# A hybrid decoder trunk on one core: in the recurrence's first two steps, where ScalarE copies the next q and f, and where VectorE does the next front

## The chip, the cores and the metric

The kernel runs on one core of one Trainium2 chip. The metric is the device time of the whole program in microseconds (us), lower is better, with the median of three runs as the kernel's time. A profile was taken of one further execution.

## The reference, cut to what matters

Two layers; each has a mixer with two branches that read the same input: sliding-window attention, and a gated linear recurrence (HGRN2) with four heads of 128 x 128 state. There is one prompt of 2048 tokens and a batch of eight samples of eight tokens each, and every sample comes with recurrence states of its own.

```python
def _hgrn2(q, f_logit, i_in, lb, s0):
    ...
    def step(S, blk):
        qc, gc, kc, vc = blk
        G = jnp.cumsum(gc, axis=1)
        diff = G[:, :, None] - G[:, None, :]
        decay = jnp.exp(jnp.where(causal, diff, NEG_INF))
        A = jnp.einsum('bthd,bshd,btshd->bhts', qc, kc, decay)
        o = jnp.einsum('bhts,bshv->bthv', A, vc) + jnp.einsum('bthd,bhdv->bthv', qc * jnp.exp(G), S)
        G_last = G[:, -1]
        S_new = jnp.exp(G_last)[..., None] * S + jnp.einsum(
            'bshd,bshv->bhdv', kc * jnp.exp(G_last[:, None] - G), vc)
        return S_new, o
```

## The kernel before, in words

Each layer has three phases, one after the other with a barrier between them: attention, recurrence, output. Each phase writes one program per engine, in the order in which the code stands; semaphores join the engines. An instruction that waits holds up all that stands behind it on its engine.

The recurrence runs over 17 tiles of tokens: tile 0 holds the 64 tokens of the eight samples, tiles 1 to 16 the prompt. For a tile, TensorE (PE) computes four projections q, f, g and v of 24 matmuls each into the four banks of `Z` (`project`), and turns q and f (`transpose_qf`) after ScalarE has copied them to `zqf` (`copy_z`, line 1002). ScalarE and VectorE then make the gates' logarithms and their running sum `G` (`front_log`, `front_exp`, `front`), and the levels of `A` are made by VectorE, ScalarE, GpSimd (POOL) and PE in turn (`middle`, `level`). Behind the levels come the "ends" of a tile: VectorE writes `kh`, ScalarE takes the exponentials of `kh` and `qG` (lines 1050 and 1051), POOL multiplies both (lines 964 and 965), and PE turns `kh` (line 1358). ScalarE copies the result to `khT` (line 1056).

Tile 0 has a way of its own. PE's order there is: the projection of f of tile 1, the turning of `kh`, eight products of `A` with `v` (line 1435), half of g of tile 1, `transpose_qf(1)`, samples 0 and 1, the other half of g, samples 2 and 3, v of tile 1, q of tile 2, samples 4 to 7, f of tile 2. For one sample (`sample_states`) PE reads its old state in eight matmuls (line 1410) and makes its update in eight more (line 1420). VectorE masks `khT` to a sample's rows (`state_rows`, line 1241) and then blends update and old state (`new_dec`, line 1247). The old states lie in four buffers `s_dec`; SyncE (SP) stores and loads them in this order:

```python
for b in range(4):
    store_state(b)
for b in range(4):
    sp.wait_ge(sd_st[b], 16)
    load_state(b + 4)
```

`store_state(b)` waits until `new_dec(b)` is done, so that the load for sample 4 stands behind the stores of samples 0 to 3. PE's reading of sample 4 waits for that load.

Of the kernel before, what the change touches and what calls it, by code (L numbers as in the profile page):

```python
# [30 lines left out]
DEC_BATCH, DEC_SEQ = 8, 8  # L31
# [39 lines left out]
def wait(eng, sem, value):  # L71

    if not isinstance(value, int) or value > 0:
        eng.wait_ge(sem, value)
# [751 lines left out]
def recurrence_phase(nc, layer, C, dram, S, weights, following):  # L826
# [4 lines left out]
    with ExitStack() as ctx:  # L831
# [37 lines left out]
        def first(n):  # L869

            return isinstance(n, int) and n == 0

        def tokens(n):

            return DEC if first(n) else P

        def passed(n):

            return 0 if first(n) else NL * n + len(DEC_LEVELS) - NL
# [6 lines left out]
        with nc.Block() as block:  # L886
# [106 lines left out]
            def _(act):  # L993
                def split_high(n, k):
                    act.wait_ge(S["x_in0"], 16 * n + 16)
                    wait(act, S["z_v"], n - 1)
                    act.activation(xh[k][:, :, :], xraw[:, :, :], ACT.Copy).then_inc(S["x_high"], 1)

                def copy_z(n):
                    act.wait_ge(S["z_f"], n + 1)  # L1000
                    wait(act, S["qf_ps"], n)
                    act.activation(zqf[:, :, :], Z[:, 0:1024], ACT.Copy).then_inc(S["zqf_sb"], 1)
# [6 lines left out]
                def front_log(n):  # L1009

                    act.wait_ge(S["z_g"], n + 1)
                    act.wait_ge(S["qf_ps"], n + 1)
                    wait(act, S["logf_done"], n)
                    act.activation(expo[:, :, :], FG, ACT.Abs).then_inc(S["act_abs"], 1)
                    act.wait_ge(S["act_abs"], n + 1)
                    act.activation(expo[:, :, :], expo[:, :, :], ACT.Exp, scale=-1.0).then_inc(S["act_exp"], 1)
                    act.wait_ge(S["act_exp"], n + 1)
                    act.activation(expo[:, :, :], expo[:, :, :], ACT.Ln, bias=1.0).then_inc(S["act_ln"], 1)
                    wait(act, S["ends_prod"], n)
                    wait(act, S["diag_ps"], n)  # L1020
                    act.activation(qT[:, :, :], banks["q"], ACT.Copy).then_inc(S["qT_sb"], 1)
# [12 lines left out]
                def middle(n, levels, after=lambda l: None):  # L1034
                    for l, h in enumerate(levels):
                        act.wait_ge(S["level_sub"], passed(n) + l + 1)
                        act.activation(E[l % 2][:, :], E[l % 2][:, :], ACT.Exp).then_inc(S["level_exp"], 1)  # L1037
                        if l == 3:
                            copy_uT(n - 1)
                        after(l)  # L1040
                    act.wait_ge(S["khx_done"], n + 1)
                    wait(act, S["o_done"], n)
                    if first(n):
                        last = G[:, :, 0:DEC].rearrange("p g (b t) -> p g b t", t=DEC_SEQ)[:, :, :, DEC_SEQ - 1]
                        act.activation(dec_s[:, :, :], last, ACT.Exp)
                    else:
                        wait(act, S["state_done"], n)
                        act.activation(decay[:, :], G[:, :, P - 1], ACT.Exp)
                    used = kh[:, :, 0:tokens(n)]
                    act.activation(used, used, ACT.Exp)  # L1050
                    act.activation(qG[:, :, :], G[:, :, :], ACT.Exp).then_inc(S["ends_exp"], 1)

                def copy_khT(n):
                    act.wait_ge(S["khT_ps"], n + 1)
                    wait(act, S["update_ps"], n)
                    act.activation(khT[:, :], M[:, :], ACT.Copy).then_inc(S["khT_sb"], 1)
# [11 lines left out]
                def copy_uT(n):  # L1068
                    act.wait_ge(S["uT_ps"], n + 1)
                    act.activation(mixT[:, :, :], M[:, :], ACT.Copy).then_inc(S["uT_out"], 1)  # L1070
# [12 lines left out]
                def around_first(l):  # L1083
                    if l == 0:
                        split_high(2, 0)
                    if l == 2:
                        copy_z(1)

                middle(0, DEC_LEVELS, around_first)
                copy_khT(0)  # L1090
                front_log(1)
                front_exp(1)
# [31 lines left out]
            def _(dve):  # L1124
# [112 lines left out]
                def state_rows(b):  # L1237

                    if b >= 2:
                        dve.wait_ge(S["sd_mm"], b - 1)  # L1240
                    dve.tensor_scalar(kE[b % 2][:, :], khT[:, :], C["batch_rows"][:, b:b + 1], None, ALU.mult)\
                        .then_inc(S["rows_done"], 1)

                def new_dec(b):
                    dve.wait_ge(S["sd_mm"], b + 1)
                    for g in range(GH):
                        op = dve.scalar_tensor_tensor(out=s_dec[b % 4][:, g, :], in0=s_dec[b % 4][:, g, :],
                                                      scalar=dec_s[:, g, b:b + 1], in1=LV[b % 2][:, g * DK:(g + 1) * DK],
                                                      op0=ALU.mult, op1=ALU.add)
                    op.then_inc(S["sd_done"], 1)  # L1250
# [26 lines left out]
                dve.wait_ge(S["khT_sb"], 1)  # L1277
                state_rows(0)
                state_rows(1)
                for b in range(4):  # L1280
                    new_dec(b)
                    state_rows(b + 2)
                front(1, 1)
                for b in range(4, DEC_BATCH):
                    new_dec(b)
                    if b + 2 < DEC_BATCH:
                        state_rows(b + 2)
# [784 lines left out]
```

## Time and profile before

| | us |
|---|---|
| median of three runs | 3034.33 |
| lowest and highest of them | 3031.73, 3035.17 |
| the profiled execution's own time | 3030.23 |
| its span, first to last instruction | 3028.5 |
| TensorE busy in the span | 2803.7 (93%) |
| VectorE busy | 1589.3 (52%) |
| ScalarE busy | 1009.5 (33%) |
| POOL busy | 1058.1 (35%) |

The profile gives for every instruction its start and duration from the start of the span, and for an idle time of its engine what ended it. PEclk is the clock that was granted to TensorE as a share of the full 2.4 GHz; 0.50 is 1.2 GHz. The mean of it over the span is 0.956.

### The profile page before, as it was taken

How to read it: one execution, taken by the hardware profiler on the slowest of the kernel's cores; microseconds unless marked ns; L12 is line 12 of the kernel's file. 1: busy time of each engine (PE TensorE's matmuls, PEld its weight loads, DVE VectorE, ACT ScalarE, POOL GpSimd, SP SyncE). 2: the span in 40 equal slices, each digit the busy share in tenths (PEclk: the TensorE clock that was granted, in tenths of full speed). 3: DMA queues.
4: the chain of work that ended last, by engine and by line, in shares of the span. 5: the costliest groups of instructions: out<-in, count | busy, mean ns of one | idle time of the engine just before them, and what ended most of it. 6: DMA issues, size and time to landing. Idle time of an engine off the chain costs nothing. (4 is left out here: it accounts for less than half of the span.)

```text
span 3028.5 us, 42852 instructions
## 1 busy us (share of the span) xinstructions
PE 2803.7 (93%) x15186; PEld 2351.7 (78%) x15186; DVE 1589.3 (52%) x3037; ACT 1009.5 (33%) x2154; POOL 1058.1 (35%) x940
## 2 busy tenths in 40 slices
PE   6999868999999699999959999589999997899998
PEld 5777647888888578888757877478888886788887
DVE  4566654676667552222236666646676665622222
ACT  3333332444444331111123333424444443311111
POOL 1212112555555443333212221125555544433332
PEclk9999978999999799999979999789999997999999
DMA  4111221000000422222141111310000004121121
GB/s 156 42 42 36 102 69 53 28 21 24 21 28 14 175 68 76 79 88 88 59 163 51 32 41 66 110 53 22 28 21 24 21 21 155 67 68 68 68 68 45
DMA packets 94463, 186.18 MB, mean 61 GB/s; under 512 B 10640, under 2 KB 55952, under 8 KB 92304
## 3 DMA queue, kind: packets, MB, share of 16 engines
q1 hardware_dynamic: 94384, 185.14, 18.4%
q8 instruction: 48, 0.79, 0.1%
q14 instruction: 31, 0.25, 0.0%
HBM read 135.10 MB, written 51.90 MB: 62 GB/s over the span
## 5 line engine op out<-in xcount | busy, mean ns | idle before, releaser
L103 PE MATMUL r_Z<-w_rec_high,w_rec_xh 128*128 128x512 f32 x1088 | 446.3, 410 | 38.7 <-POOL w_rec_xl L942 30.3
L103 PE MATMUL r_Z<-w_rec_high,w_rec_xl 128*128 128x512 f32 x1088 | 430.7, 396 | 0.0
L103 PE MATMUL r_Z<-w_rec_low,w_rec_xh 128*128 128x512 f32 x1088 | 429.8, 395 | 0.0
L103 PE MATMUL a_Z<-w_attn_high,w_attn_xh 128*128 128x512 f32 (+1 forms) x816 | 303.1, 371 | 0.0
L103 PE MATMUL a_Z<-w_attn_low,w_attn_xh 128*128 128x512 f32 (+1 forms) x816 | 291.7, 358 | 0.0
L103 PE MATMUL a_Z<-w_attn_high,w_attn_xl 128*128 128x512 f32 (+1 forms) x816 | 290.9, 357 | 0.0
L951 POOL TENSOR_TENSOR r_qE<-r_qT,r_E 128x256 f32<-128x256 f32 x230 | 188.7, 820 | 282.2 <-ACT r_E L1037 157.1
L1344 PEld LDWEIGHTS r_LV<-r_qE,r_kE 128*128 128x128 f32 x1840 | 249.1, 207 | 48.6 <-POOL r_kE L951 27.3
L1344 PE MATMUL r_LV<-r_qE,r_kE 128*128 128x64 f32 x1840 | 249.8, 290 | 32.3 <-POOL r_kE L951 22.7
L103 PEld LDWEIGHTS r_Z<-w_rec_high,w_rec_xh 128*128 128x128 f32 x1088 | 209.2, 192 | 78.7 <-issue 40.2
L1184 DVE COPY_PREDICATED r_A<-levels,r_LV 128x256 f32<-128x256 int32 x230 | 121.5, 528 | 245.6 <-issue 161.9
L103 PEld LDWEIGHTS r_Z<-w_rec_high,w_rec_xl 128*128 128x128 f32 x1088 | 207.8, 191 | 46.4
L103 PEld LDWEIGHTS r_Z<-w_rec_low,w_rec_xh 128*128 128x128 f32 x1088 | 209.1, 192 | 39.4
L1037 ACT ACTIVATE r_E<-r_E 128x512 f32<-128x512 f32 x230 | 145.3, 633 | 267.5 <-DVE r_E L1173 267.5
L951 POOL TENSOR_TENSOR r_kE<-r_kT,r_E 128x256 f32<-128x256 f32 x230 | 210.9, 917 | 0.0
L1762 PE MATMUL o_MX<-w_out_high,o_mh 128*128 128x512 f32 x512 | 202.5, 396 | 2.8 <-DVE o_hb L1702 2.8
L1762 PE MATMUL o_GT<-w_out_high,o_hh 128*128 128x512 f32 x512 | 200.9, 392 | 3.0 <-issue 3.0
L1762 PE MATMUL o_MX<-w_out_high,o_ml 128*128 128x512 f32 x512 | 200.1, 391 | 0.0
L1762 PE MATMUL o_GT<-w_out_high,o_hl 128*128 128x512 f32 x512 | 199.5, 390 | 0.0
L1762 PE MATMUL o_GT<-w_out_low,o_hh 128*128 128x512 f32 x512 | 199.2, 389 | 0.0
L1762 PE MATMUL o_MX<-w_out_low,o_mh 128*128 128x512 f32 x512 | 199.2, 389 | 0.0
L1726 DVE SCALAR_TENSOR_TENSOR o_th<-o_th,o_PL 128x1024 f32<-128x1024 f32 x34 | 41.5, 1222 | 290.2 <-PE o_PL L1762 290.2
(253 smaller groups left out, 5645.9 us busy)
## 6 DMA issues: line engine op xcount, KB each, us to landing
w_attn_xraw<-dram_xT SPq DMA_DIRECT2D x34, 512.0 KB, 3.6
r_xraw<-dram_xT SPq DMA_DIRECT2D x34, 512.0 KB, 3.4
o_mraw<-dram_mixT SPq DMA_DIRECT2D x34, 512.0 KB, 4.4
dram_y_all<-o_hb SPq DMA_DIRECT2D x34, 512.0 KB, 2.9
w_rec_whole<-dram_w_in SPq DMA_DIRECT2D x16, 1024.0 KB, 12.3
w_attn_whole<-dram_w_in SPq DMA_DIRECT2D x16, 640.0 KB, 7.9
dram_mixT<-a_mixT SPq DMA_DIRECT2D x136, 64.0 KB, 2.1
dram_mixT<-r_u SPq DMA_DIRECT2D x34, 256.0 KB, 2.0
```

The costliest lines, as they stand in the source:

```text
L103: mm = pe.matmul(out, a[:, c, :], b[:, c, :], start=(first and c == chunks[0] and a is xh and b is wh), stop=(last and c == chunks[-1] and ...
L951: op = pool.tensor_tensor(to, halves(flat(q_or_k), h)[half], halves(E[i][:, :], h)[half], ALU.mult)
L1037: act.activation(E[l % 2][:, :], E[l % 2][:, :], ACT.Exp).then_inc(S["level_exp"], 1)
L1184: dve.copy_predicated(to, mask, src).then_inc(S["level_took"], 1)
L1344: mm = pe.matmul(LV[i][:, 64 * g:64 * g + 64], kE[i][:, g * P:(g + 1) * P], qE[i][:, g, :], start=True, stop=True)
L1726: dve.scalar_tensor_tensor(out=th[:, :], in0=th[:, :], scalar=1.0, in1=PL[:, :], op0=ALU.add, op1=ALU.mult).then_inc(S["blend"], 1)
L1762: mm = pe.matmul(out[0][:, out[1]], a[:, c, :], w, start=(c == 0 and a is high and b is wh), stop=(c == chunks - 1 and a is low))
```

## The change

In the first step of the recurrence (tile 0), ScalarE's copy of q and f of tile 1 stood behind the third level's exponential, ahead of the tile's ends. It now stands behind the ends. On VectorE the whole front of tile 1 stood behind the new states of samples 0 to 3; it now stands behind those of samples 0 and 1. Nothing is added or removed.

```diff
                 def around_first(l):
                     if l == 0:
                         split_high(2, 0)
-                    if l == 2:
-                        copy_z(1)
 
                 middle(0, DEC_LEVELS, around_first)
+                copy_z(1)
                 copy_khT(0)
                 front_log(1)
                 front_exp(1)
...
                 state_rows(0)
                 state_rows(1)
-                for b in range(4):
+                for b in range(2):
                     new_dec(b)
                     state_rows(b + 2)
                 front(1, 1)
-                for b in range(4, DEC_BATCH):
+                for b in range(2, DEC_BATCH):
                     new_dec(b)
                     if b + 2 < DEC_BATCH:
                         state_rows(b + 2)
```

ScalarE's instructions from the last exponential of tile 0's levels (L1037) to the copy of `khT`, before:

```order
132 L1037 ACTIVATE r_E<-r_E 128x512 x2
133 L1002 ACTIVATE r_zqf<-r_Z 128x1024
134 L1045 ACTIVATE r_dec_s<-r_G 128x32
135 L1050 ACTIVATE r_kh<-r_kh 128x4x64
136 L1051 ACTIVATE r_qG<-r_G 128x512
137 L1056 ACTIVATE r_khT<-r_M 128x512
```

The same place now:

```order
132 L1037 ACTIVATE r_E<-r_E 128x512 x2
133 L1045 ACTIVATE r_dec_s<-r_G 128x32
134 L1050 ACTIVATE r_kh<-r_kh 128x4x64
135 L1051 ACTIVATE r_qG<-r_G 128x512
136 L1002 ACTIVATE r_zqf<-r_Z 128x1024
137 L1056 ACTIVATE r_khT<-r_M 128x512
```

The copy from `Z` (L1002) has moved behind the three exponentials of the ends and stays ahead of the copy of `khT`.

VectorE's instructions from the samples' first row masks, before (the front begins with L1130):

```order
303 L1241 TENSOR_SCALAR r_kE<-r_khT,batch_rows 128x512 x2
304 L1247 SCALAR_TENSOR_TENSOR r_s_dec<-r_s_dec,r_dec_s,r_LV 128x128 x4
305 L1241 TENSOR_SCALAR r_kE<-r_khT,batch_rows 128x512
306 L1247 SCALAR_TENSOR_TENSOR r_s_dec<-r_s_dec,r_dec_s,r_LV 128x128 x4
307 L1241 TENSOR_SCALAR r_kE<-r_khT,batch_rows 128x512
308 L1247 SCALAR_TENSOR_TENSOR r_s_dec<-r_s_dec,r_dec_s,r_LV 128x128 x4
309 L1241 TENSOR_SCALAR r_kE<-r_khT,batch_rows 128x512
310 L1247 SCALAR_TENSOR_TENSOR r_s_dec<-r_s_dec,r_dec_s,r_LV 128x128 x4
311 L1241 TENSOR_SCALAR r_kE<-r_khT,batch_rows 128x512
312 L1130 SCALAR_TENSOR_TENSOR r_lsig<-r_Z,r_expo 128x1024
```

The same place now, where every line of VectorE's program has a number lower by one:

```order
305 L1240 TENSOR_SCALAR r_kE<-r_khT,batch_rows 128x512
306 L1246 SCALAR_TENSOR_TENSOR r_s_dec<-r_s_dec,r_dec_s,r_LV 128x128 x4
307 L1240 TENSOR_SCALAR r_kE<-r_khT,batch_rows 128x512
308 L1129 SCALAR_TENSOR_TENSOR r_lsig<-r_Z,r_expo 128x1024
...
320 L1156 SCALAR_TENSOR_TENSOR r_G<-r_ones,r_lsig 128x128 x4
321 L1246 SCALAR_TENSOR_TENSOR r_s_dec<-r_s_dec,r_dec_s,r_LV 128x128 x4
322 L1240 TENSOR_SCALAR r_kE<-r_khT,batch_rows 128x512
323 L1246 SCALAR_TENSOR_TENSOR r_s_dec<-r_s_dec,r_dec_s,r_LV 128x128 x4
```

The new states of samples 2 and 3 (rows 308 and 310 of before) stand behind the front's scans now (rows 321 and 323).

## Rows read from the trace of the kernel before

**Rows 1.** The page's part 1: busy time, share and instructions of each engine

```profile
PE 2803.7 (93%) x15186; PEld 2351.7 (78%) x15186; DVE 1589.3 (52%) x3037; ACT 1009.5 (33%) x2154; POOL 1058.1 (35%) x940
```

**Rows 2.** Timeline of PE, layer 0: start us, us, engine, line, operation, [idle <-releaser]

```profile
457.45 0.39 PE L103 MATMUL r_Z<-w_rec_high,w_rec_xl 128*128 128x512 f32 x1
461.94 1.12 PE L1358 MATMUL r_M<-ident,r_kh 128*128 128x128 f32 x4 [4.10 <-POOL r_qG L965]
462.85 1.81 PE L1435 MATMUL r_O<-r_A,r_v 128*128 128x64 f32 x8
464.42 0.77 PE L103 MATMUL r_Z<-w_rec_high,w_rec_xh 128*128 128x512 f32 x1
...
468.62 0.60 PE L1326 MATMUL r_Z<-ident,r_zqf 128*128 128x128 f32 x4
469.05 0.60 PE L1328 MATMUL r_Z<-ident,r_zqf 128*128 128x128 f32 x4
...
472.98 0.47 PE L103 MATMUL r_Z<-w_rec_high,w_rec_xh 128*128 128x512 f32 x1
...
475.83 0.95 PE L1410 MATMUL r_O<-r_qG,r_s_dec 128*128 128x8 f32 x8
476.64 1.14 PE L1420 MATMUL r_LV<-r_v,r_kE 128*128 128x128 f32 x8
477.61 0.96 PE L1410 MATMUL r_O<-r_qG,r_s_dec 128*128 128x8 f32 x8
...
490.30 0.95 PE L1410 MATMUL r_O<-r_qG,r_s_dec 128*128 128x8 f32 x8
```

**Rows 3.** Timeline of ScalarE, layer 0

```profile
444.92 0.63 ACT L1037 ACTIVATE r_E<-r_E 128x512 f32<-128x512 f32 x1 [2.50 <-DVE r_E L1173]
457.88 1.02 ACT L1002 ACTIVATE r_zqf<-r_Z 128x1024 f32<-128x1024 f32 x1 [12.33 <-PE r_Z L103]
...
478.17 1.06 ACT L1018 ACTIVATE r_expo<-r_expo 128x1024 f32<-128x1024 f32 x1
```

**Rows 4.** Timeline of VectorE, layer 0

```profile
445.14 0.62 DVE L1204 TENSOR_TENSOR r_kh<-r_G 128x64 f32<-128x64 f32 x4
...
477.81 1.12 DVE L1247 SCALAR_TENSOR_TENSOR r_s_dec<-r_s_dec,r_dec_s,r_LV 128x128 f32<-128x128 f32 x4 [3.03 <-PE r_LV L1420]
...
479.60 1.12 DVE L1247 SCALAR_TENSOR_TENSOR r_s_dec<-r_s_dec,r_dec_s,r_LV 128x128 f32<-128x128 f32 x4 [0.27 <-PE r_LV L1420]
480.64 0.48 DVE L1241 TENSOR_SCALAR r_kE<-r_khT,batch_rows 128x512 f32<-128x512 f32 x1
481.04 1.22 DVE L1130 SCALAR_TENSOR_TENSOR r_lsig<-r_Z,r_expo 128x1024 f32<-128x1024 f32 x1
...
488.28 1.37 DVE L1157 TENSOR_TENSOR_SCAN r_G<-r_ones,r_lsig 128x128 f32<-128x128 f32 x4
```

**Rows 5.** SP's issues from 481.17 us, and the landing of the first of them

```profile
481.17 2.41 SPq L898 DMA_DIRECT2D r_s_dec<-dram_state  x4
...
DMA to landing us min/median/max: 3.1/3.1/3.1
```

**Rows 6.** Windows: stretch, its us, busy us (instructions) of PE, PEld, DVE, ACT, POOL, then PEclk

```profile
1979.92:1984.00 4.08, 0.00 (x0) 0.00 (x0) 0.00 (x0) 1.99 (x4) 1.99 (x3) 0.86 0.00 0
...
490.30:497.90 7.60, 7.30 (x65) 7.13 (x64) 4.42 (x15) 0.49 (x2) 0.00 (x0) 1.00 0.24 69
...
442.89:450.27 7.38, 6.40 (x30) 6.03 (x31) 4.32 (x9) 0.63 (x1) 3.35 (x4) 0.54 0.01 3
...
1014.43:1036.90 22.47, 20.35 (x89) 19.10 (x90) 12.63 (x21) 5.59 (x10) 13.23 (x14) 0.50 0.85 327
...
42.28:46.00 3.72, 3.72 (x34) 3.56 (x36) 0.00 (x0) 1.50 (x3) 1.37 (x1) 1.00 0.06 11
```

**Rows 7.** Timeline of PE, two other idle times and what ended them

```profile
442.89 1.49 PE L1344 MATMUL r_LV<-r_qE,r_kE 128*128 128x64 f32 x8 [3.74 <-POOL r_kE L951]
...
42.28 0.74 PE L671 MATMUL a_SC<-ident,a_qk 128*128 128x128 f32 x5 [2.86 <-POOL a_qk L288]
```

## The prediction

> **What bounds the kernel now.** I read the page first. PE is busy for 2803.7 of 3028.5 us [rows 1]. Whatever shortens or lengthens the run must therefore open or close a wait of PE, or change the speed at which PE works. Then I read the timeline of each engine around the edited place, once for each layer, and last the windows with the granted clock, since an idle PE can lose clock as well as time.
>
> In layer 0, PE's projection of f ends with the matmul that starts at 457.45. PE then stands idle for 4.10 us, until the turning of `kh` at 461.94 [rows 2]. The releaser is POOL's product for `qG`. POOL was late because ScalarE held its ends behind `copy_z(1)`, and that copy started at 457.88, once the projection of f was complete [rows 3]. The reader should see that the ends' own data had been ready since 445.14 + 0.62 = 445.76 [rows 4], and ScalarE was free at 445.55 [rows 3]. Layer 1 has the same hole: PE busy 0.00 of 4.08 us from 1979.92 [rows 6].
>
> Everything behind that hole is one chain on PE: `kh`, `A` with `v`, half of g, `transpose_qf(1)`, samples 0 and 1, the other half of g, samples 2 and 3, v, q, and samples 4 to 7 from 490.30 [rows 2]. The stretch of samples 4 to 7 has 7.30 us busy in 7.60, at a clock of 1.00 [rows 6]. So before the change, nothing there waits for long.
>
> **Edit 1, the copy behind the ends: what it gives.** From the end of `copy_z(1)` (457.88 + 1.02 = 458.90) to the turning of `kh` (461.94), exponentials and products take 3.0 us. Begun at 445.76 they are done near 449, or a little later if POOL still has its last level to finish. That is well before PE's f is complete at 457.8, so the work that hides them is that projection; without it they would cost 3.0 us, as they do now. Matmuls of this kind start 0.23 us apart at full clock (2.85 us for 12, from 472.98 to 475.83 [rows 2]), so PE turns `kh` at 457.68 instead of 461.94: 4.26 us earlier.
>
> The hole has a second price, the clock. The four turns took 462.85 - 461.94 = 0.91 us, where four turns at full clock take 469.05 - 468.62 = 0.43. The eight products with `v` took 464.42 - 462.85 = 1.57 us, where eight matmuls with the same weight loads take 476.64 - 475.83 = 0.81. The half of g took 468.62 - 464.42 = 4.20 us against 2.85. Together: 0.48 + 0.76 + 1.35 = 2.6 us [rows 2]. **Edit 1 gives 4.26 + 2.6 = 6.9 us per layer**, up to the samples.
>
> What the moved copy itself delays: it still starts at 457.88 with the end of f, and ends at 458.90 [rows 3]; the turning of q and f wants it at 457.68 + 0.43 + 0.81 + 2.85 = 461.8. The copy of `khT` (half as wide, so at most the same 1.02) and VectorE's first mask (0.48 [rows 4]) follow by 460.4; PE wants that mask behind two turnings and a reading, at 461.8 + 0.86 + 0.81 = 463.5. Both are covered, with 2.9 us or more to spare. SP's and POOL's queues keep their order.
>
> **Edit 2, the front behind two states.** In the old order the front began at 481.04, though ScalarE's logarithm that it needs was done at 478.17 + 1.06 = 479.23 [rows 3, 4]. In the new order it begins when the logarithm is there: 479.26 - 6.9 = 472.4. It can gain 1.8 us at most, and nobody on PE asks for it so early: PE next needs it for f of tile 2, behind samples 4 to 7. I cost this gain at nothing.
>
> What now stands behind the front: `new_dec(2)` and `new_dec(3)`. Behind `new_dec(3)` stands SP's store of sample 3, and behind that the load of sample 4, for which PE waits. The steps:
>
> - The front lasts from 481.04 to 488.28 + 1.37 = 489.65, so 8.6 us, its own wait for ScalarE included [rows 4]. It ends at 472.4 + 8.6 = 481.0.
> - `new_dec(2)` to the mask behind it 480.64 - 479.60 = 1.04 us; a mask to the next instruction 481.04 - 480.64 = 0.40; `new_dec(3)` 1.12 [rows 4]. So `new_dec(3)` is done at 483.5.
> - Before, it was done at 479.60 + 1.12 = 480.72; the load of sample 4 was issued at 481.17, 0.45 later, and landed 3.1 us after that [rows 4, 5]. Now it lands at 483.5 + 0.45 + 3.1 = 487.1.
> - PE comes to sample 4 at 490.30 - 6.9 = 483.4 [rows 2].
>
> **PE stands idle for 3.7 us** in a place where it did not wait. Net of both edits, sample 4 starts 6.9 - 3.7 = 3.2 us earlier. Bounds of the wait: none if the load landed 3.7 us sooner, which its row excludes; up to 1 us more if the stores of samples 2 and 3, now 1.04 + 0.40 = 1.4 us apart instead of 479.60 - 477.81 = 1.8, crowd it.
>
> **What the new wait does to the clock.** This is the dear part. After the idle times of 4.10 and 3.74 us the rows show half clock: 0.91 us for four turns [rows 2], and 0.54 over 442.89 to 450.27 [rows 6, 7]. After one of 2.86 us it stayed at 1.00 [rows 6, 7]. With 3.7 us I take the fall as near certain. The Trainium skill ("TensorE: Matmul & The Clock Gate", Why this matters for your kernels) warns of long idle gaps between bursts of matmuls for this reason, and this trace agrees (3.74 us fell, 2.86 did not).
>
> Once low, does it come back inside samples 4 to 7? The nearest row says no: from 1014.43 to 1036.90 PE was busy for 20.35 of 22.47 us with small matmuls (levels, turns, diagonal, output) and had 0.50 all the time [rows 6]. So all four samples would run at half clock. A sample costs 0.81 + 0.97 = 1.78 us now (475.83 to 476.64 to 477.61); at half clock eight matmuls like the reading took 1.57 and eight like the update 2 x 0.91 = 1.82, so 3.39 [rows 2]. **Four samples: + 4 x 1.61 = 6.4 us.** Bounds: 5.8 if the clock falls 0.6 us late (0.54 instead of 0.50 over 7.38 us [rows 6]), 7.1 for plain doubling. I take off 0.3: 6.1. Then f of tile 2 begins at half clock, where it now begins at full: like half of g, **+1.35 us**, bounds 0.5 and 2.8.
>
> **The sum.** Per layer: -6.9 + 3.7 + 6.1 + 1.35 = +4.2 us; two layers +8.5. What follows (output of the samples, tile 1, the loops) is a chain that starts from that f, so it shifts as a whole. Against the profiled execution's 3030.2 us: 3038.7. That execution lies 4.1 below the median; against the median of 3034.3 the time is **3042.8 us**.
>
> **Rivals.**
> 1. *The new wait is there, but the clock stays up.* For it: 2.86 us did no harm, and 3.7 may be 3.3. Against: 3.74 did. It needs a load that lands half a microsecond or more sooner. Price: -3.2 per layer, 3028 us. This is the rival of the other side. It decides from a wait somewhere between 2.86 and 3.74 us downwards. Chance 0.07.
> 2. *The clock falls and comes back within the four samples.* Then half clock costs some 2 to 3 us of the 6.1 and nothing of f: -3.2 + 2.5 = -0.7 per layer, 3033 us. Against it speaks the 22.47 us stretch [rows 6]; for it, that a sample's update is eight matmuls of 128 columns without a pause, which is more work than a level's. Chance 0.13. The Trainium skill ("TensorE: Matmul & The Clock Gate", Part 1) would have it so: sustained matmuls bring the full clock back soon, whatever their size. By that rule the time is this rival's, 3033 us; the long stretch at 0.50 in this trace disagrees, and the sum above goes by the row.
> 3. *The load is in time after all*, because VectorE or SP come earlier than I have it: edit 1's gain alone, -6.9 x 2, 3020 us. It asks for 3.7 us that the code's order does not leave. Chance 0.03.
> 4. *The gain of edit 1 is smaller*, for another wait takes POOL's place (the copy of `khT`, the masks). Sample 4 comes later, and its wait shrinks by as much; the clock decides again. 3036 to 3046. Chance 0.07, inside my range.
>
> The forecast itself has 0.70; its own range is 3038 to 3049, from the bounds above (+2.2 to +7.4 per layer, rounded).
>
> **How the numbers follow.** A measurement of this kernel can tell about 0.2%, 6 us. The forecast is slower by 0.28%, so part of its own range lies within 6 us: of its 0.70, I put 0.54 to slower, 0.16 to same. Rival 2 is same; rival 1 is at the border, half faster and half same; rival 3 faster; rival 4 and the rest split. Faster 0.10, same 0.32, slower 0.58. The range of 8 in 10 reaches from rival 2, with some of rival 1's side, to the upper bound: 3030 to 3048.
>
> **What the profile would show.** Right: no idle PE ahead of the turning of `kh`, in both layers, with 12 matmuls of g in 2.85 us behind it; ScalarE's copy behind the `qG` exponential; `new_dec(2)` right behind the scans near 481; PE idle for 3 to 5 us ahead of the reading of sample 4, ended by the load; half clock from there, four samples in 13 to 14 us instead of 7.60. Wrong: a clock of 1.00 over those samples (rivals 1 or 2), or no idle time there (rival 3).

## The result and the profile after

The changed kernel takes 3043.22 us (median of 17 runs, 3040.31 to 3048.37), the kernel before 3032.92 us (median of 17, 3029.05 to 3042.70). The ratio is 1.0032, with a 95% interval of 1.0024 to 1.0039: slower by about 10 us. The profiled execution took 3043.56 us, with a span of 3041.8.

The page's part 1 for the changed kernel, to be held against [rows 1]:

```profile
PE 2814.3 (93%) x15186; PEld 2360.5 (78%) x15186; DVE 1587.0 (52%) x3037; ACT 1010.2 (33%) x2154; POOL 1063.5 (35%) x940
```

PE has the same 15186 matmuls and is busy 10.6 us longer. Nothing was added to it, so the same work ran at a lower speed. That already points at the clock, more than at waiting.

PE's timeline of layer 0, the places of [rows 2] (line numbers behind the edit are lower by one):

```profile
457.22 0.60 PE L1357 MATMUL r_M<-ident,r_kh 128*128 128x128 f32 x4
457.66 1.00 PE L1434 MATMUL r_O<-r_A,r_v 128*128 128x64 f32 x8
458.47 0.48 PE L103 MATMUL r_Z<-w_rec_high,w_rec_xh 128*128 128x512 f32 x1
...
461.33 0.60 PE L1325 MATMUL r_Z<-ident,r_zqf 128*128 128x128 f32 x4
...
486.58 1.28 PE L1409 MATMUL r_O<-r_qG,r_s_dec 128*128 128x8 f32 x8 [3.43 <-DMA r_s_dec<-dram_state]
487.72 2.06 PE L1419 MATMUL r_LV<-r_v,r_kE 128*128 128x128 f32 x8
489.56 1.71 PE L1409 MATMUL r_O<-r_qG,r_s_dec 128*128 128x8 f32 x8
491.13 2.05 PE L1419 MATMUL r_LV<-r_v,r_kE 128*128 128x128 f32 x8
```

The first row has no idle time ahead of it any more, and from the turning of `kh` to that of f it is 4.11 us instead of 6.68. That is edit 1's gain. In its place stands 3.43 us of waiting ahead of sample 4, ended by the load of its state. From there a sample takes 3.42 us (489.56 to 492.98, the next reading) instead of 1.78.

VectorE and SP at the same place (for [rows 4] and [rows 5]):

```profile
479.21 1.37 DVE L1156 TENSOR_TENSOR_SCAN r_G<-r_ones,r_lsig 128x128 f32<-128x128 f32 x4
480.49 1.10 DVE L1246 SCALAR_TENSOR_TENSOR r_s_dec<-r_s_dec,r_dec_s,r_LV 128x128 f32<-128x128 f32 x4
481.51 0.48 DVE L1240 TENSOR_SCALAR r_kE<-r_khT,batch_rows 128x512 f32<-128x512 f32 x1
481.90 1.12 DVE L1246 SCALAR_TENSOR_TENSOR r_s_dec<-r_s_dec,r_dec_s,r_LV 128x128 f32<-128x128 f32 x4
...
483.47 2.38 SPq L898 DMA_DIRECT2D r_s_dec<-dram_state  x4
```

The reader should see the line of dependence: scans, new state of sample 2, mask, new state of sample 3 (done at 483.02), then at 483.47 the issue of the load for which PE waits until 486.58.

Windows over samples 4 to 7 and the projection of f behind them, and over the samples in layer 1 (last three numbers: PEclk, then DMA share and GB/s), for [rows 6]:

```profile
486.58:500.30 13.72, 13.43 (x64) 13.15 (x65) 4.42 (x15) 0.48 (x2) 0.00 (x0) 0.53 0.35 99
500.31:507.73 7.42, 7.42 (x24) 5.87 (x25) 2.22 (x7) 0.49 (x1) 0.00 (x0) 0.73 0.37 108
2015.60:2029.17 13.57, 13.28 (x64) 13.00 (x65) 4.41 (x15) 0.48 (x2) 0.00 (x0) 0.53 0.36 104
```

The four samples took 7.60 us at a clock of 1.00 before. They take 13.7 now, at 0.53.

### The profile page after: what moved, and what is told of

It reads as the page before. It is cut to its first block and busy times, and to the rows that moved or that the text cites. A ratio compares the mean times of both kernels' runs of the same rounds, so it can differ in the third digit from the quotient of the medians.

```text
span 3041.8 us, 42852 instructions
## 1 busy us (share of the span) xinstructions
PE 2814.3 (93%) x15186; PEld 2360.5 (78%) x15186; DVE 1587.0 (52%) x3037; ACT 1010.2 (33%) x2154; POOL 1063.5 (35%) x940
## 5 line engine op out<-in xcount | busy, mean ns | idle before, releaser
L1037 ACT ACTIVATE r_E<-r_E 128x512 f32<-128x512 f32 x230 | 145.3, 633 | 266.4 <-DVE r_E L1172 266.4
```

## The experiments

Each comparison is with the kernel before, run beside it on the same chip. Its median there was 3032.83 us for the first four kernels and 3034.33 us for the last four. There is one trace of each kernel, with the two layers as two cases in it.

### Edit 1 alone

The copy stands behind the ends as in the changed kernel; the front stays where it was.

```diff
-                    if l == 2:
-                        copy_z(1)
 
                 middle(0, DEC_LEVELS, around_first)
+                copy_z(1)
                 copy_khT(0)
```

> Only the copy of q and f stands behind the ends of tile 0; the front stays behind the new states of four samples. Theory (the copy gains, the late new states lose): TensorE's idle 4.1 us ahead of the turning of kh goes, with the 2.6 us that it cost in clock, and the load for sample 4 is in time, so 6.9 us less per layer: 13.8 us less than before, ratio 0.9955, with samples 4 to 7 at full clock in about 7.6 us. Rival (the moved copy is itself what costs, for what waits for it): ratio 1.001 or more.

Measured: 3019.32 us, ratio 0.9956 (0.9944 to 0.9968), 13.5 us less. PE starts the samples 4 to 7 without a wait, and the windows show full clock in both layers:

```profile
482.99:490.59 7.60, 7.30 (x65) 7.13 (x64) 4.42 (x15) 0.49 (x2) 0.00 (x0) 1.00 0.24 69
2005.20:2012.80 7.60, 7.30 (x65) 7.13 (x64) 4.42 (x15) 0.49 (x2) 0.00 (x0) 1.00 0.24 69
```

So the moved copy costs nothing up to the samples and gives what its sum says. The loss comes from edit 2. The size of the gain is less certain than the two medians make it look: the profiled execution of this kernel was the slowest of its six (3023.26 us), and its span is only 7.0 us below that of before (3021.5 against 3028.5). Where it lost the rest is told below, in the part on why the prediction was right.

### Edit 2 alone

```diff
-                for b in range(4):
+                for b in range(2):
                     new_dec(b)
                     state_rows(b + 2)
                 front(1, 1)
-                for b in range(4, DEC_BATCH):
+                for b in range(2, DEC_BATCH):
```

> Only the front stands behind the new states of two samples instead of four; the copy of q and f stays where it was. Theory: new_dec(3) ends near 490.4 us in layer 0, the load of sample 4 lands near 494, TensorE wants it at 490.3: an idle time of 3.7 us, half clock over four samples (6.1 us) and into the next projection (1.9 us): 11.7 us more per layer, 23 us more in all, ratio 1.0077. Rival (the new wait arises only because edit 1 brings TensorE to the samples early): no wait here, ratio 1.000.

Measured: 3055.84 us, ratio 1.0076 (1.0064 to 1.0088), 23 us more. The wait is there without edit 1, and has the same size (3.46 us in layer 1), as PE's timeline shows for layer 0:

```profile
491.31 1.29 PE L1410 MATMUL r_O<-r_qG,r_s_dec 128*128 128x8 f32 x8 [3.37 <-DMA r_s_dec<-dram_state]
```

This is as the chain has it: VectorE's front waits for TensorE's g, so that everything from g to sample 4 shifts together, with edit 1 or without. The two edits add up: -13.5 + 23.0 = +9.5 us against the measured +10.3.

### The front behind three new states

```diff
-                for b in range(2):
+                for b in range(3):
                     new_dec(b)
                     state_rows(b + 2)
                 front(1, 1)
-                for b in range(2, DEC_BATCH):
+                for b in range(3, DEC_BATCH):
```

> The changed kernel with the front behind three new states instead of two, so that one new state and one mask less stand behind it, 1.4 us. Theory (the size of the wait decides, by the clock): TensorE's wait for the load of sample 4 is 3.43 - 1.4 = 2.0 us and the clock stays at 1.00, so samples 4 to 7 take 7.6 us and not 13.7: per layer -6.9 + 2.1 = -4.8 us, 9.6 us less than before, ratio 0.997. Rival (the clock has nothing to do with it, the cost is proportional to the wait): 1.4 us less per layer than the changed kernel, ratio near 1.0023. If the clock falls even at 2.0 us, ratio near 1.002 as well, but with 0.50 granted over the samples.

Measured: 3039.49 us, ratio 1.0020 (1.0011 to 1.0028). My number was wrong, and by the clock. The wait shrank to 2.09 us as worked out, but the clock fell all the same, about 2 us after PE had gone on (in the changed kernel it was 0.7 us). The row of the wait, a row behind the fall, and the window over the four samples:

```profile
488.35 1.06 PE L1409 MATMUL r_O<-r_qG,r_s_dec 128*128 128x8 f32 x8 [2.09 <-DMA r_s_dec<-dram_state]
...
491.58 2.05 PE L1419 MATMUL r_LV<-r_v,r_kE 128*128 128x128 f32 x8
...
488.35:500.75 12.40, 12.11 (x64) 11.83 (x65) 4.41 (x15) 0.49 (x2) 0.00 (x0) 0.59 0.38 109
```

The first sample ran at full clock, the other three mostly at half. Layer 1 did the same (2.10 us of waiting, 12.27 us at 0.59). The time alone would also fit the rival, a cost in proportion to the wait; the granted clock tells them apart. In attention a longer idle time of 2.86 us had left the clock at 1.00 [rows 6, 7]. So the length of the idle time does not decide alone in this trace.

### The loads of samples 4 and 5 early

The changed kernel, with SP's order changed:

```diff
-                for b in range(4):
+                for b in range(2):
                     store_state(b)
                 for b in range(4):
+                    if b == 2:
+                        store_state(2)
+                        store_state(3)
                     sp.wait_ge(sd_st[b], 16)
                     load_state(b + 4)
```

> The changed kernel, with SP's loads of samples 4 and 5 issued behind the stores of samples 0 and 1 instead of behind all four stores. Theory (TensorE waits for the load alone, not for VectorE): no idle time ahead of sample 4, at most 1 us ahead of sample 6 and 1.5 us ahead of sample 7, clock at 1.00: -6.9 + 1 to 2 per layer, 10 to 12 us less than before, ratio 0.9962. Rival (what hurts is that the new states are late, whatever the loads do): a wait of about 3 us stays, ended by VectorE, ratio above 1.001.

Measured: 3025.88 us, ratio 0.9979 (0.9970 to 0.9987), 7 us less. The wait ahead of sample 4 is gone and the clock is at 1.00 in both layers:

```profile
483.02:490.94 7.92, 7.57 (x65) 7.21 (x64) 4.85 (x17) 0.49 (x2) 0.00 (x0) 1.00 0.63 183
2001.61:2010.38 8.77, 7.84 (x65) 7.28 (x64) 4.85 (x17) 0.48 (x2) 0.00 (x0) 1.00 0.62 182
```

The new states are as late as in the changed kernel, and do no harm. What hurt was the load queued behind them. The gain is less than the 10 to 12 us expected, although the four samples lose only 0.3 and 1.2 us to the later loads. Part of the rest lies behind the samples. From the turning of their output to the end of v of tile 2 this kernel took 34.17 us in layer 0 and 33.93 in layer 1, against 32.48 and 32.52 before: 3.1 us in all. Some 2 us stay open. That stretch is looked at again below.

### The projection of f of tile 2 ahead of samples 4 to 7

The changed kernel, with work for PE in the place of the wait:

```diff
                 project(2, 0, "q")
-                sample_states(4, DEC_BATCH)
                 project(2, 0, "f")
+                sample_states(4, DEC_BATCH)
```

> The changed kernel, with TensorE's projection of f of tile 2 ahead of samples 4 to 7 instead of behind them. Its 5.5 us are longer than the 3.43 us for which TensorE waited for the load of sample 4. Theory: no wait, no fall of the clock, samples 4 to 7 in 7.6 us: both edits then give the same as edit 1 alone, 13.8 us less than before, ratio 0.9955. Rival (something else in the late front costs too): above 0.998.

Measured: 3019.66 us, ratio 0.9948 (0.9935 to 0.9962). The samples run at full clock in layer 1 too (7.45 us). The late front then costs nothing that the medians can tell, as expected: the wait and what follows from it were its whole price.

```profile
488.64:496.08 7.44, 7.30 (x65) 7.13 (x64) 4.26 (x15) 0.39 (x1) 0.00 (x0) 1.00 0.27 76
```

### A wait of 2 us, and what stands behind it

The kernel with the front behind three states again. PE waits for the same load at the same place, but goes on with the projection of f.

```diff
                 project(2, 0, "q")
-                sample_states(4, DEC_BATCH)
+                pe.wait_ge(sd_in[0], 32)
                 project(2, 0, "f")
+                sample_states(4, DEC_BATCH)
```

> The kernel with the front behind three states, where TensorE waited 2.09 us and the clock fell soon after it went on. Here TensorE waits for the same load at the same place, but the projection of f of tile 2 stands behind the wait and samples 4 to 7 behind the projection. Theory (it fell because the small matmuls that follow do little in the same stretch): the clock stays at 1.00, samples in 7.6 us: -6.9 + 2.1 per layer, 9.6 us less than before, ratio 0.997. Rival (a wait of 2.1 us is long enough by itself): clock 0.50 from there, back within the projection, about 1.4 us per layer more, ratio 0.998 and a stretch at 0.50 in the trace.

Measured: 3023.64 us, ratio 0.9965 (0.9951 to 0.9979). The wait is 2.10 us, as long as the 2.09 there, and the clock stays at 1.00 over the projection and the samples. Layer 1 did the same, with a wait of 1.92 us. The rows of layer 0:

```profile
485.25 0.50 PE L103 MATMUL r_Z<-w_rec_high,w_rec_xh 128*128 128x512 f32 x1 [2.10 <-DMA r_s_dec<-dram_state]
...
485.25:490.81 5.56, 5.56 (x24) 4.62 (x25) 0.00 (x0) 0.00 (x0) 0.00 (x0) 1.00 0.37 100
490.82:498.20 7.38, 7.31 (x65) 7.11 (x63) 4.20 (x15) 0.38 (x1) 0.00 (x0) 1.00 0.26 73
```

With nearly the same wait, the clock fell where samples came next (two layers) and stayed where a projection came next (two layers). That supports what I had not reckoned with: what PE does behind the wait counts here, and not only how long it waited. It isn't proof, for the place of the wait in time differs too (it began at 486.26 there and at 483.15 here), and no run moved it by itself.

### The full wait, and then the projection

The same edit of PE's order on the changed kernel itself.

> The changed kernel with its full wait of 3.4 us for the load of sample 4, and then the projection of f of tile 2 ahead of samples 4 to 7. Theory (the wait costs 3.4 us, the half clock over the four samples 6.1 us): the clock falls as before but comes back within the projection, at 1.4 to 2 us, and the samples take 7.6 us: -6.9 + 3.4 + 1.7 = -1.8 per layer, 3.6 us less than before, ratio 0.9988. Rival (the wait itself is the whole cost): as the changed kernel, ratio 1.0032.

Measured: 3030.40 us, ratio 0.9990 (0.9981 to 0.9999). The wait is 3.42 us (3.53 in layer 1), the clock falls, and is back within the projection, which takes 7.2 us instead of 5.5; the samples run at 1.00:

```profile
488.21 0.50 PE L103 MATMUL r_Z<-w_rec_high,w_rec_xh 128*128 128x512 f32 x1 [3.42 <-DMA r_s_dec<-dram_state]
...
488.21:495.39 7.18, 7.17 (x24) 5.75 (x25) 0.00 (x0) 0.00 (x0) 0.00 (x0) 0.76 0.29 82
495.40:502.80 7.40, 7.31 (x65) 7.11 (x63) 4.22 (x15) 0.38 (x1) 0.00 (x0) 1.00 0.25 71
```

This splits the loss. PE waits as long as in the changed kernel, and yet the time is below that of before. The difference between 1.0032 and 0.9990, some 13 us or 6.4 us per layer, is what half clock over the four samples costs, against 13.7 - 7.4 = 6.3 in the windows. The intervals of the two ratios leave about 2 us per layer of room on the first figure; the windows are the sharper evidence.

### The turning of the samples' output ahead of f

Edit 1 alone, with the 4.2 us for which PE waits behind that turning filled by the projection:

```diff
-                project(2, 0, "f")
                 pe.wait_ge(S["oT_sb"], 1)
                 for g in range(GH):
                     t = pe.transpose(M[0:DEC, g * DK:(g + 1) * DK], u[:, g * DEC:(g + 1) * DEC], C["ident"][:, :])
                 t.then_inc(S["o_done"], 1)
+                project(2, 0, "f")
```

> Edit 1 alone, and the turning of the samples' output (L1450) ahead of the projection of f of tile 2, so that this projection stands in the 4.2 us for which TensorE waits between that turning and tile 1's first level. Theory: 6.9 us per layer of edit 1, 4.2 us of the wait, and up to 3 us for the levels behind it, whose clock no longer falls (8.9 us now, partly bound by POOL): 22 to 28 us less than before, ratio 0.991 to 0.993. Rival (the chain of squares, root and POOL sets tile 1's start whatever TensorE does): ratio 0.9955 as in edit 1 alone, since TensorE then waits behind the projection instead.

Measured: 3010.19 us, ratio 0.9918 (0.9905 to 0.9932), 24 us less than before. PE goes from the turning to tile 1's first levels with hardly a wait, and at full clock for the first two of them:

```profile
490.89 0.60 PE L1448 MATMUL r_M<-ident,r_u 128*64 128x128 f32 x4
...
496.79 1.00 PE L1343 MATMUL r_LV<-r_qE,r_kE 128*128 128x64 f32 x8
498.07 1.08 PE L1343 MATMUL r_LV<-r_qE,r_kE 128*128 128x64 f32 x8 [0.28 <-issue]
500.36 1.10 PE L1343 MATMUL r_LV<-r_qE,r_kE 128*128 128x64 f32 x8 [1.21 <-POOL r_kE L951]
```

So the wait of 4.2 us was filled, in both layers. The up to 3 us that I gave for the clock did not come: it fell all the same, only later (0.59 from 500.36 to 506.83). From f of tile 2 to the end of v of tile 2 this kernel takes 33.6 us with the turning ahead of f, where the kernel before takes 38.0 (497.91 to 535.92): 4.4 us less, hardly more than the wait. The two layers give 8.8 us on top of edit 1's 13.5, near the 24 measured. This version beats both kernels.

## Why the prediction was right, step by step

- **Edit 1 gives 6.9 us per layer: right, up to the samples.** With it alone sample 4 started at 482.99 instead of 490.30, 7.3 us earlier in layer 0. Of these, 0.46 us stood there ahead of the edited place (457.42 instead of 457.88 at ScalarE's copy), which leaves 6.85. The medians of the whole program differ by 13.5 us, against 13.8. Part of that agreement is luck, for the profiled execution lost much of the gain again behind the samples: 1.9 us in the next stretch of layer 0 and 3.3 us in the loops over the other tiles, both told below.
- **The wait for sample 4's load, 3.7 us: right, 0.3 too long.** It was 3.43 and 3.50 us. The new state of sample 3 was done at 483.02 instead of 483.5; the whole trace stood 0.46 us earlier there (ScalarE's copy of q and f began at 457.42 instead of 457.88).
- **Sample 4 starts 3.2 us earlier than before: right.** It started at 486.58 instead of 490.30, 3.72 with those 0.46 us in it, so 3.3.
- **The clock falls and stays low over four samples, +6.1: right.** 13.72 us instead of 7.60 is 6.1, and the comparison with the kernel that has the full wait and then the projection gives 6.4. The bounds around it hold a slip that changes nothing here: -6.9 + 3.7 + 5.8 + 0.5 is +3.1 per layer (2.8 with the 0.3 taken off), not the +2.2 of the lower end. Rival 2, and with it the rule of the Trainium skill ("TensorE: Matmul & The Clock Gate", Part 1) that sustained matmuls bring the clock back, did not happen here: PE was busy for 13.43 of 13.72 us at 0.53.
- **f of tile 2 at half clock, +1.35: too small.** From the start of f to the turning behind it, it was 507.74 - 500.31 = 7.43 us instead of 5.53, so 1.9.
- **"It shifts as a whole": this step was off.** From that turning to the end of the projection of v of tile 2 it took longer in the changed kernel, as these two windows show (first before, then after):

```profile
503.44:535.92 32.48, 25.68 (x129) 22.65 (x128) 18.85 (x36) 12.42 (x25) 18.59 (x19) 0.79 0.08 23
```

```profile
507.74:541.44 33.70, 26.35 (x129) 23.17 (x128) 19.23 (x36) 12.41 (x25) 18.32 (x19) 0.75 0.07 21
```

It has the same 129 matmuls and 1.2 us more, at a lower mean clock (0.75 instead of 0.79). Layer 1 gives the same pair (32.52 and 33.74). With edit 1 alone the two layers differ from each other:

```profile
496.12:530.50 34.38, 27.01 (x129) 23.62 (x128) 19.25 (x36) 12.43 (x25) 18.35 (x19) 0.75 0.07 23
2018.33:2050.82 32.49, 25.65 (x129) 22.61 (x128) 18.89 (x36) 12.43 (x25) 18.52 (x19) 0.79 0.07 25
```

PE is idle for some 4 us in this stretch (in all kernels but the one with the turning ahead of f), and the clock falls there in all of them. How long it then stays low differs, and even one kernel shows both lengths. So I counted this stretch as fixed, and it is not; but whether its 1.2 us belong to the change, or to where the clock happened to come back in one profiled execution, no run here shows.

Summed with what was measured: -3.3 + 6.1 + 1.9 + 1.2 = +5.9 us per layer against my +4.2, and 11.8 in all. The two profiled executions differ by 13.3 us; 3.3 of it come from the loops over the other tiles (below) and -1.8 from elsewhere. The medians differ by 10.3. So the prediction of 3042.8 met 3043.22 as to its mechanism (the hole closed, the new wait, the half clock), while the agreement to half a microsecond is luck. Its sum of +8.5 us stands against +10.3 measured, two terms are 0.5 to 1.2 us per layer too small, and the median of before came out 1.4 us below the one that I started from.

The rivals: rival 1 and rival 3 did not occur. The point that I gave for rival 1 (it decides from a wait between 2.86 and 3.74 us downwards) was wrong for this place, since the clock fell at 2.09. Rival 4 did not occur, for edit 1 had its full gain up to the samples.

## What to carry to other kernels

Before moving work ahead of an instruction on one engine, follow what is queued behind that instruction on the other engines: here two small vector operations held a store, the store held a load, and TensorE waited for the load. A short new wait of TensorE can cost more than itself: here 2.09 us with small matmuls behind it, and 3.43 us, were paid again in clock over the next samples. Ahead of a large projection a wait of 2.10 us left the clock at 1.00, and one of 3.42 us cost only 1.7 us beyond itself. Where TensorE must wait, look for independent large matmuls in its own program that can be put there: that turned the loss of 10 us into a gain of 15, and with edit 1 alone, at another wait of the same step, made its gain of 13.5 one of 24.

## What was unexpected in the hardware

The first point is the fall of the clock behind a wait of only 2.09 us, told above.

The second lies in the loops over tiles 3 to 16, whose code the change does not touch. The windows over 14 tiles of layer 0, before and after:

```profile
535.92:1006.41 470.49, 470.10 (x2802) 413.47 (x2800) 317.57 (x686) 224.09 (x433) 247.98 (x265) 1.00 0.06 22
```

```profile
541.44:1013.87 472.43, 470.60 (x2802) 413.43 (x2800) 316.31 (x687) 224.18 (x433) 251.40 (x265) 1.00 0.07 22
```

The clock is 1.00 in both, and POOL is busy 3.4 us longer. In the trace of the changed kernel several of the tiles, in layer 0 every second one from the fifth on, take 33.9 us instead of 33.6: 9 in the two layers, against none in the trace of before. (The first and the last of the 14 tiles of a layer take 33.8 to 33.9 us in every kernel and are not counted.) Such tiles are there in the traces of edit 1 alone (10), of edit 2 alone (10), of the front behind three states (10), of the early loads (3), of f ahead of the samples (11) and of the turning ahead of f (10). There is none in the two kernels with a wait ahead of f. So they don't go with the edits in any plain way. A pair of operations differs. Before, VectorE and then POOL in the same tile:

```profile
676.86 0.99 DVE L1173 TENSOR_TENSOR r_E<-r_G 128x256 f32<-128x256 f32 x1
...
676.83 0.74 POOL L951 TENSOR_TENSOR r_qE<-r_qT,r_E 128x256 f32<-128x256 f32 x1 [0.30 <-ACT r_E L1037]
```

After:

```profile
682.43 0.41 DVE L1172 TENSOR_TENSOR r_E<-r_G 128x256 f32<-128x256 f32 x1
...
682.40 1.04 POOL L951 TENSOR_TENSOR r_qE<-r_qT,r_E 128x256 f32<-128x256 f32 x1 [0.30 <-ACT r_E L1037]
```

The two start within 0.03 us of each other in both traces, and one of them takes 0.3 to 0.6 us longer. In the first trace it is VectorE's operation, in the second POOL's. In all 28 tiles of both traces the tile is a long one (33.8 us or more) where POOL's operation is the slow one (0.98 to 1.04 us), and a short one where VectorE's is (0.98 or 0.99 us). That they hold each other up is what the durations suggest; no run here took one of them away, and what decides between the two stays open. The Trainium skill ("GPSIMD Engine Reference", 1. Specifications) says that POOL's interfaces to SBUF are shared with VectorE, and that the two contend when VectorE's instruction has two SBUF inputs, as the subtraction in these rows has. The rows agree with it, without showing the cause. It is worth 1.9 us in layer 0 and 1.3 in layer 1 of the profiled execution.
